# Two constant loads on another queue, conditioning sums three chunks ahead, and attention scores kept in one PSUM bank, in a two-block transformer kernel

## The chip, the core and the metric

The kernel runs as one launch on one core of one Trainium2 chip. The metric is the device time of that launch in microseconds; the median of three runs of the kernel before is 2705.99 us (2705.83 to 2706.22). Its five engines work on their own instruction streams and meet only through semaphores: TensorE (PE) for matmuls, VectorE (DVE), ScalarE (ACT), GpSimd (POOL) and the queue engine SP.

## The reference

Two transformer blocks follow each other on 256 tokens of width 2048, in fp32. The change is all in the first one. Cut to what matters:

```
mod = silu(c) @ w_ada + b_ada                      # 6 parts of 2048 ("conditioning")
shift1, scale1, gate1, shift2, scale2, gate2 = split(mod, 6)
h = rms_norm(x, norm1_w) * (1 + scale1) + shift1
u_pool, q, k, v, g_a, g_b = split(h @ w_in)        # 1024 x 4, 2048 x 2 columns
y_a = multiscale_pool(u_pool, w_pool, pool_scale) @ w_a_up
q, k = rms_norm(q, q_norm_w), rms_norm(k, k_norm_w)      # per head of 128, 8 heads
y_b = stick_breaking_attention(q, k, v) @ w_b_up
x = x + gate1 * ((sigmoid(g_a) * y_a + sigmoid(g_b) * y_b) @ w_o)
x = x + gate2 * (square(relu(h2 @ w_ff1)) @ w_ff2)       # h2: second norm and modulation

# attention of one head: z = q.k / sqrt(128), mask: key before query
log_beta = log_sigmoid(z);  l = where(mask, log_beta - z, 0)
a = where(mask, exp(log_beta + reverse_cumsum(l) - l), 0);  out = a @ v
```

## The kernel before, in words

**Weights.** All weights stream from HBM once, as pieces of 512 KB ("items"), in the order of `weight_plan`, through six slots (`RAW`, four, and `RAWX`, two). SP issues them; a slot is refilled when DVE has finished with what it held. There are two sorts. A weight chunk is 256 rows by 512 columns: ACT copies it to a rounded tile `WH` (line 993), DVE subtracts to get the rest `WL` (line 1359), and PE multiplies (line 588) with the activations, which are split the same way into `AH` and `AL`: two row blocks, two token tiles, three products each, 12 matmuls of 512 columns a chunk. `WH` and `WL` have three slots each, so ACT may copy chunk j+2 once PE is through with chunk j-1. A conditioning item is no matmul: DVE adds it, scaled by one column of silu(c), to the accumulator `ACC` (line 1367).

**Ticks.** Every engine runs one loop over the chunk number j (848 in all), and all its other work hangs at a fixed j, in the order written: on ACT and DVE `feed(j + 2)` (copies, subtractions and conditioning items up to chunk j+2), `evac` (reading out a finished PSUM bank), `quarter`, `side`; on PE the chunk and then `side`. No scheduler reorders anything: an instruction that waits holds up all that is behind it on its engine.

**The first projection** is chunks 0 to 127. Its modulation (scale1, shift1) is needed first and comes in four quarters of 512 columns. `quarter(q)` on PE sums `ACC` over partitions with two matmuls against ones; DVE takes the diagonals, adds bias and forms scale and shift (7 instructions); ACT writes `AH` of four row blocks and the unrounded values (8 instructions); `quarter_low(q)` on DVE writes `AL` (4 instructions). To have work before all quarters are there, `PIECES` splits the 16 column blocks of w_in into pieces (column block, first chunk, last chunk): first those that need only quarter 0, and so on. `SUMS` says before which chunk PE does the sum of each quarter. Before the change quarter q is summed before chunk 20, 40, 60 and first used at chunk 22, 42, 62.

**Banks.** A piece accumulates in a pair of PSUM banks (one bank for each token tile, t = 0 and 1). Column block 0 has a pair of its own until its last piece; the others alternate between two pairs. When a piece ends at chunk e, tile 0 is read out at j = e+1 and tile 1 at j = e+2 (`ended`), by ACT for a block's first piece, by DVE (as an addition) for its later ones. A piece that begins must wait for the readout of the piece that had its banks before (`bank_free`), tile by tile.

**Beside the projection**, from given chunks on: the pooling (`POOL0`); the q and k norms, whose sums of squares DVE makes, whose reciprocal roots POOL makes (`rsqrt`, 15 small dependent instructions, lines 1929 and 1934) and which DVE applies (`qk_norm`, at `QKN0`); and the attention, one head every two chunks from `STK0` on (`stick`). Stage 0 of a head transposes q and k, stage 2 makes scores Z in bank 5 and from them softplus terms on ACT and DVE (`E1`, `E2`), stage 4 makes the exponent E in bank 6: the scores again, the mask, and two matmuls that form the sums over later keys; ACT takes exp, and stage 6 multiplies with v. POOL's instruction stream holds loads as well: `ST` (the mask constants, tile `SX`) and the gate bias (1 MB, tile `G`) wait for the pooling to end and stand ahead of `rsqrt`.

Of the kernel before, what the change touches and what calls it, by code (L numbers as in the profile page):

```python
# [26 lines left out]
POOL0 = 69  # L27
QKN0 = 77
STK0 = 83
# [106 lines left out]
def weight_plan(I):  # L136
# [46 lines left out]
    head = spread(head, [ada1[2], ada1[3], ada1[4]], 62, 176)  # L183
    for q in range(1, 4):
        a, n = 20 * (q - 1), 18
# [3 lines left out]
        plan += head[a + n:a + 20]  # L189
# [105 lines left out]
class Blocks:  # L295


    def __init__(self):
# [49 lines left out]
def program(nc, I, C, out):  # L348
# [3 lines left out]
    with ExitStack() as ctx:  # L352
# [24 lines left out]
        NT = sb("NT", [128, 3, 16])  # L377
# [134 lines left out]
        s_sga, s_stat = sem("gate_a"), sem("st_landed")  # L512
# [44 lines left out]
        RSQ = {("qk", a): 15 * (a + 1) for a in range(2)}  # L557
        RSQ |= {("rope", r): 15 * (r + 3) for r in range(8)}
        RSQ |= {("mix", m): 15 * (m + 11) for m in range(4)}
        RSQ["attn"] = 15 * 15  # L560

# [23 lines left out]
        def _(e):  # L585
# [404 lines left out]
        def _(e):  # L990
# [46 lines left out]
            def evac(q, t):  # L1037
# [18 lines left out]
                elif name == "in1":  # L1056
# [3 lines left out]
                    e.wait_ge(s_stO, 8)  # L1060
# [91 lines left out]
            def stick(h, s):  # L1152
# [10 lines left out]
                elif s == 2:  # L1163
# [3 lines left out]
                    af(e1, PS[:, 5, 0:384], ACT.Abs).then_inc(s_stx, 1)  # L1167
# [4 lines left out]
                elif s == 4:  # L1172
# [3 lines left out]
                    af(e3, PS[:, 6, 0:384], ACT.Exp).then_inc(s_st3, 1)  # L1176
# [164 lines left out]
            for j in range(NW + 3):  # L1341
# [14 lines left out]
        def _(e):  # L1356
# [80 lines left out]
            def ada_made(b, g, n):  # L1437
# [183 lines left out]
            def qk_norm(a, t):  # L1621
                e.wait_ge(s_rs, RSQ["qk", a])
# [5 lines left out]
            def stick(h, s):  # L1628
                b = h % 2
                e1, e2 = E1[:, b, :], E2[:, b, :]  # L1630
                if s == 2:
# [6 lines left out]
                    stt(e2, PS[:, 5, 0:384], 0.0, e1, ALU.max, ALU.add).then_inc(s_ste, 1)  # L1638
# [180 lines left out]
            def side(j):  # L1819
# [10 lines left out]
                if j in (QKN0, QKN0 + 1, QKN0 + 5, QKN0 + 6):  # L1830
                    qk_norm((j - QKN0) // 5, (j - QKN0) % 5)
# [64 lines left out]
            for j in range(NW + 3):  # L1896
# [13 lines left out]
                if j in SUMS[1:]:  # L1910
                    quarter(SUMS.index(j))
                if j - 1 in SUMS[1:]:
                    quarter_low(SUMS.index(j - 1))
# [3 lines left out]
        def _(e):  # L1917
# [136 lines left out]
```

## Time and profile before

| what | us |
|---|---|
| median of 3 runs | 2705.99 |
| profiled execution, its own time | 2697.7 |
| its span, first to last instruction | 2695.9 |
| PE busy | 2545.9 (94%) |
| DVE busy | 2005.1 (74%) |
| ACT busy | 1271.9 (47%) |
| POOL busy | 285.3 (11%) |
| mean granted clock of TensorE | 0.981 |

Times on the timeline are microseconds from the start of the span. The first projection covers about 42 to 502 us of it. The busy time of PE counts matmuls that overlap, so a chunk of 12 matmuls that each show 0.39 us takes 2.72 us from the start of one chunk to that of the next. An fp32 matmul that is not of the rounded kind leaves two records.

### The profile page before, as it was taken

What the parts mean: (1) busy time and instruction counts of PE and PEld (TensorE: products, weight loads), DVE (VectorE), ACT (ScalarE), POOL (GpSimd) and SP (SyncE); (2) the same over time, 40 slices, a digit from 0 to 9 for tenths busy, and PEclk for the clock granted to TensorE, in tenths of its full rate; (3) what the DMA queues carried; (4) which work ended last, traced back from release to release, by engine and by line L of the source; (5) the groups of instructions that cost most, each with busy time, mean ns of one, the idle gap of its engine ahead of it and who ended that gap; (6) DMA issues with size and microseconds to landing.
All of it is one profiled execution on the core that took longest, in us unless ns stands there. A gap on an engine that the chain in (4) does not pass through costs nothing.

```text
span 2695.9 us, 36321 instructions
## 1 busy us (share of the span) xinstructions
PE 2545.9 (94%) x14339; PEld 2215.0 (82%) x14339; DVE 2005.1 (74%) x2238; ACT 1271.9 (47%) x1584; POOL 285.3 (11%) x340
## 2 busy tenths in 40 slices
PE   5999789999899999999998999978989999999998
PEld 4777678878899889988976888767789988999897
DVE  6788667899886888797887777977775566565556
ACT  4534376434454444444435554445545444444442
POOL 0000220202002020202020001461000000020000
PEclk9999899999999999999999999999999999999999
DMA  8888657988798979897965645566567777776664
GB/s 317 310 306 305 208 189 264 334 308 294 253 346 266 351 261 351 264 357 258 349 212 177 187 133 149 187 197 218 175 221 221 226 232 229 227 219 194 189 187 148
DMA packets 297882, 661.80 MB, mean 245 GB/s; under 512 B 20736, under 2 KB 20832, under 8 KB 296944
## 3 DMA queue, kind: packets, MB, share of 16 engines
q1 hardware_dynamic: 294704, 648.12, 72.6%
q0 software_dynamic: 3008, 11.36, 1.2%
q8 instruction: 114, 1.87, 0.3%
q14 instruction: 56, 0.46, 0.0%
HBM read 657.30 MB, written 2.10 MB: 245 GB/s over the span
## 4 chain that ended last, share of the span: by engine, by line
PE 77%; DVE 11%; issue 4%; ACT 4%; DMA 3%; POOL 1%; SPq 0%; DVEq 0%; ACTq 0%; POOLq 0%
PE PS L588 77%; DVE WL L1359 3%; DVE ACC L1367 3%; ACT WH L993 2%; DMA RAW<-in_w_o 1%; DVE UQ L1359 1%; DMA RAW<-in_w_in 1%; DVE hn L1364 1%; PE PS L591 0%; ACT L993 0%; ACT UQ L993 0%; DVE acc L1359 0%; DMA RAW<-in_w_out 0%; DMA RAW<-in_w_ada 0%; POOL NT L1929 0%
## 5 line engine op out<-in xcount | busy, mean ns | idle before, releaser
L1359 DVE TENSOR_TENSOR WL<-RAW,WH 128x1024 fp32r<-128x1024 f32 x573 | 714.5, 1248 | 406.9 <-ACT WH L993 405.6
L993 ACT ACTIVATE WH<-RAW 128x1024 fp32r<-128x1024 f32 x573 | 607.2, 1060 | 862.1 <-PE PS L588 665.7
L588 PE MATMUL PS<-WH,AH 128*128 128x512 f32 x2052 | 817.6, 398 | 43.3 <-DVE AL L1359 23.5
L588 PE MATMUL PS<-WH,AL 128*128 128x512 f32 x2052 | 804.3, 392 | 0.0
L588 PE MATMUL PS<-WL,AH 128*128 128x512 f32 x2052 | 804.0, 392 | 0.0
L588 PE MATMUL PS<-BH,WH 128*128 128x256 f32 x2048 | 574.8, 281 | 6.1 <-DVE BL L1359 6.1
L588 PE MATMUL PS<-BH,WL 128*128 128x256 f32 x2048 | 571.4, 279 | 0.0
L588 PE MATMUL PS<-BL,WH 128*128 128x256 f32 x2048 | 571.3, 279 | 0.0
L588 PEld LDWEIGHTS PS<-WH,AH 128*128 128x128 f32 x2052 | 389.1, 190 | 132.7 <-DVE WL L1359 31.6
L588 PEld LDWEIGHTS PS<-WH,AL 128*128 128x128 f32 x2052 | 388.2, 189 | 83.6
L588 PEld LDWEIGHTS PS<-WL,AH 128*128 128x128 f32 x2052 | 389.0, 190 | 78.8 <-issue 1.0
L588 PEld LDWEIGHTS PS<-BH,WH 128*128 128x128 f32 x2048 | 384.4, 188 | 9.7 <-DVE BL L1359 9.2
L588 PEld LDWEIGHTS PS<-BH,WL 128*128 128x128 f32 x2048 | 385.0, 188 | 0.0
L588 PEld LDWEIGHTS PS<-BL,WH 128*128 128x128 f32 x2048 | 383.1, 187 | 0.5
L1367 DVE SCALAR_TENSOR_TENSOR ACC<-RAW,CS,ACC 128x1024 f32<-128x1024 f32 x259 | 330.9, 1278 | 2.2 <-DMA RAW<-in_w_ada 1.3
L1950 POOL PARTITION_ALL_REDUCE ACC<-ACC x72 | 156.6, 2258 | 1319.8 <-DVE ACC L1367 1319.8
L993 ACT ACTIVATE WH<-RAWX 128x1024 fp32r<-128x1024 f32 x144 | 152.7, 1060 | 206.7 <-PE PS L588 137.5
L1359 DVE TENSOR_TENSOR WL<-RAWX,WH 128x1024 fp32r<-128x1024 f32 x144 | 179.5, 1247 | 60.2 <-ACT WH L993 59.6
L1359 DVE TENSOR_TENSOR WL<-RAWY,WH 128x1024 fp32r<-128x1024 f32 x96 | 117.7, 1226 | 78.8 <-ACT WH L993 78.8
L993 ACT ACTIVATE WH<-RAWY 128x1024 fp32r<-128x1024 f32 x96 | 101.9, 1062 | 137.4 <-PE PS L588 133.8
L1367 DVE SCALAR_TENSOR_TENSOR ACC<-RAWX,CS,ACC 128x1024 f32<-128x1024 f32 x101 | 128.8, 1277 | 0.9 <-DMA RAWX<-in_w_ada 0.5
L588 PE MATMUL PS<-WX,AH 128*128 128x512 f32 x248 | 78.1, 396 | 2.0 <-DVE AL L1359 2.0
(240 smaller groups left out, 2061.5 us busy)
## 6 DMA issues: line engine op xcount, KB each, us to landing
RAW<-in_w_ff SPq DMA_DIRECT2D x335, 512.0 KB, 4.5
RAW<-in_w_ada SPq DMA_DIRECT2D x278, 512.0 KB, 5.3
RAW<-in_w_in SPq DMA_DIRECT2D x197, 512.0 KB, 4.4
RAWX<-in_w_ada SPq DMA_DIRECT2D x106, 512.0 KB, 5.4
RAWY<-in_w_ff SPq DMA_DIRECT2D x96, 512.0 KB, 4.5
RAWX<-in_w_ff SPq DMA_DIRECT2D x81, 512.0 KB, 5.2
RAWX<-in_w_in SPq DMA_DIRECT2D x43, 512.0 KB, 5.3
RAW<-in_w_out SPq DMA_DIRECT2D x32, 512.0 KB, 4.6
```

The costliest lines, as they stand in the source:

```text
L588: return e.matmul(o, l, r, start=start, stop=stop, skip_group_check=True)
L993: return e.activation(o, i, f, **kw)
L1359: return e.tensor_tensor(o, a, b, op)
L1364: return e.tensor_scalar(o, a, s1, s2, op0, op1)
L1367: return e.scalar_tensor_tensor(out=o, in0=a, scalar=s, in1=b, op0=op0, op1=op1)
L1950: e.partition_all_reduce(part, part, 128, bass.bass_isa.ReduceOp.add).then_inc(s_red, 1)
```

## The change

- `PIECES` is written anew: twelve blocks instead of eleven before the second quarter is needed, 46 pieces instead of 43. Quarters are first used at chunks 24, 44 and 64 and summed before 21, 41 and 61. The conditioning items of a quarter are spread over 20 chunks instead of 18.
- At those chunks the order within an engine's turn is changed: ACT does `feed`, `quarter`, `evac` (before: `feed`, `evac`, `quarter`); DVE does `quarter`, `feed`, `quarter_low`, `evac` (before: `feed`, `evac`, `quarter`, and `quarter_low` a chunk later).
- Pooling, norms and attention start 2, 6 and 4 chunks later. POOL makes the reciprocal roots of q and k in one chain over 32 columns instead of two over 16.
- The loads of `ST` and of the first gate bias are issued by ACT (at j = 80) instead of POOL.
- In the attention the second score matmuls go: mask and sums are added to the scores in the bank where they are, and the banks alternate (5 and 6) from head to head. The mask matmuls stand behind the wait for `E2` now.

```
-POOL0 = 69
-QKN0 = 77
-STK0 = 83
+POOL0 = 71
+QKN0 = 83
+STK0 = 87
-PIECES = ([(0, 0, 2)] + [(n, 0, 2) for n in range(1, 11)]
-          + [(0, 2, 4), (11, 0, 4)] + [(n, 2, 4) for n in (7, 8, 9, 10, 1, 2, 3)]
...
+PIECES = ([(n, 0, 2) for n in range(12)]
+          + [(0, 2, 4)] + [(n, 2, 4) for n in (7, 8, 9, 10, 11, 3, 4, 5, 6)]
...
-SUMS = (0, 20, 40, 60)
+SUMS = (0, 21, 41, 61)
...
-                    if h > 0:
-                        e.wait_ge(s_ste, 2 * h)
+                    if h > 1:
+                        e.wait_ge(s_st3, h - 1)
                     mm(Z[:, 0:256], kt[:, 0:128], qt, True, False)
...
-                    mm(E[:, 0:256], kt[:, 0:128], qt, True, False)
-                    mm(E[:, 256:384], kt[:, 128:256], qt[:, 128:256], False, False)
-                    mm(E[:, 0:128], ident, neglt, False, False)
-                    mm(E[:, 256:384], ident, neglt, False, False)
                     e.wait_ge(s_ste, 2 * h + 2)
-                    mm(E[:, 0:384], nge, e2, False, False)
-                    mm(E[:, 128:256], nones, e2[:, 256:384], False, True).then_inc(s_stE, 1)
+                    mm(Z[:, 0:128], ident, neglt, False, False)
+                    mm(Z[:, 256:384], ident, neglt, False, False)
+                    mm(Z[:, 0:384], nge, e2, False, False)
+                    mm(Z[:, 128:256], nones, e2[:, 256:384], False, True).then_inc(s_stE, 1)
...
+                if j == POOL0 + 9:
+                    e.wait_ge(s_poolB, 4)
+                    e.dma_start(ST, C["st"]).then_inc(s_stat, 16)
+                    e.dma_start(G[:, :], I["b_ada"][0:1, 2 * D:3 * D].partition_broadcast(128)).then_inc(s_gb0, 16)
...
                 feed(j + look(j))
+                if j in SUMS[1:]:
+                    quarter(SUMS.index(j))
                 for q, t in bl.ended(j):
                     evac(q, t)
-                if j in SUMS[1:]:
-                    quarter(SUMS.index(j))
...
-                if j in (QKN0, QKN0 + 1, QKN0 + 5, QKN0 + 6):
-                    qk_norm((j - QKN0) // 5, (j - QKN0) % 5)
+                if QKN0 <= j < QKN0 + 4:
+                    qk_norm((j - QKN0) // 2, (j - QKN0) % 2)
...
+                    if j in SUMS[1:]:
+                        quarter(SUMS.index(j))
                     feed(j + look(j))
+                    if j in SUMS[1:]:
+                        quarter_low(SUMS.index(j))
                     for q, t in bl.ended(j):
                         evac(q, t)
...
-            for a in range(2):
-                e.wait_ge(s_msr, 4 * a + 4)
-                rsqrt(SM[:, 40 + 16 * a:56 + 16 * a], SM[:, 8 + 16 * a:24 + 16 * a], 128)
+            e.wait_ge(s_msr, 8)
+            rsqrt(SM[:, 40:72], SM[:, 8:40], 128)
```

ACT around the first of the three sums. `WH` is the copy of a chunk, `AH` and `XT` belong to the quarter, `SG<-PS` is the readout of column block 9 (first row of it tile 0, the next tile 1). Before:

```order
L993 ACTIVATE WH<-RAW 128x1024 [waits w_used,raw1_landed]
L993 ACTIVATE SG<-PS 128x512 [waits w_used]
L993 ACTIVATE AH<-XT,MOD 128x256 [waits mod_made]
...
L993 ACTIVATE XT<-XT,MOD 128x256
L993 ACTIVATE WH<-RAW 128x1024 [waits w_used,raw3_landed]
L993 ACTIVATE SG<-PS 128x512 [waits w_used]
```

Now:

```order
L989 ACTIVATE WH<-RAW 128x1024 [waits w_used,raw1_landed]
L989 ACTIVATE SG<-PS 128x512 [waits w_used]
L989 ACTIVATE WH<-RAW 128x1024 [waits w_used,raw3_landed]
L989 ACTIVATE AH<-XT,MOD 128x256 [waits mod_made]
...
L989 ACTIVATE XT<-XT,MOD 128x256
L989 ACTIVATE SG<-PS 128x512 [waits w_used]
```

The copy of the next chunk moved ahead of the quarter. The readout of tile 1 is behind the quarter in both, but the piece that takes over its banks now begins at chunk 22, one chunk after the sum; before it began at chunk 24, four chunks after the sum.

DVE around the second sum. `UQ<-PS,UQ` is the readout of a piece (before column block 2, now column block 4), `PS<-PS,SQ` begins the quarter, `AL` is `quarter_low`. Before:

```order
L1359 TENSOR_TENSOR WL<-RAW,WH 128x1024 [waits w_hi]
L1359 TENSOR_TENSOR UQ<-PS,UQ 128x512 [waits bank_read_act,w_used]
L1359 TENSOR_TENSOR PS<-PS,SQ 128x512 [waits ada_summed]
...
L1367 SCALAR_TENSOR_TENSOR MOD<-MOD,VC 128x4 [waits mod_made]
L1367 SCALAR_TENSOR_TENSOR ACC<-RAW,CS,ACC 128x1024 [waits ada_acc,raw2_landed]
L1359 TENSOR_TENSOR WL<-RAW,WH 128x1024 [waits w_hi]
L1359 TENSOR_TENSOR UQ<-PS,UQ 128x512 [waits bank_read_act,w_used]
L1359 TENSOR_TENSOR AL<-XT,AH 128x256 [waits a_hi] x4
```

Now:

```order
L1359 TENSOR_TENSOR UQ<-PS,UQ 128x512 [waits bank_read_act,w_used]
L1359 TENSOR_TENSOR PS<-PS,SQ 128x512 [waits ada_summed]
...
L1367 SCALAR_TENSOR_TENSOR MOD<-MOD,VC 128x4 [waits mod_made]
L1367 SCALAR_TENSOR_TENSOR ACC<-RAW,CS,ACC 128x1024 [waits ada_acc,raw2_landed]
L1359 TENSOR_TENSOR WL<-RAW,WH 128x1024 [waits w_hi]
L1359 TENSOR_TENSOR AL<-XT,AH 128x256 [waits a_hi] x4
L1359 TENSOR_TENSOR UQ<-PS,UQ 128x512 [waits bank_read_act,w_used]
```

The readout of tile 1 stands behind the four `AL` now. At the second and third sum the piece that takes over its banks begins at chunk 42 and 62, again one chunk after the sum.

POOL from the loads of the pooling on (`qk_sums` are the sums of squares; the instruction called ISA waits for nothing). Before:

```order
L1966 DMA SX<-const_pool 128x1536 [waits a_lo]
L1967 DMA G<-in_w_pool 128x8x256
L1969 DMA SX<-const_st 128x512 [waits pool_mapped]
L1962 DMA G<-in_b_ada 128x2048
L1929 ISA
L1929 TENSOR_SCALAR NT<-SM 128x16 [waits qk_sums]
```

Now:

```order
L1969 DMA SX<-const_pool 128x1536 [waits a_lo]
L1970 DMA G<-in_w_pool 128x8x256
L1932 ISA
L1932 TENSOR_SCALAR NT<-SM 128x32 [waits qk_sums]
```

The two loads and their wait are gone from POOL, so nothing but the sums themselves is ahead of the chain.

## Rows read from the trace of the kernel before

**Rows 1.** Stretches of the first projection: us from:to, length, busy us (instructions).

```profile
229.00:247.00 18.00, 11.58 (x40) 8.41 (x39) 13.21 (x22) 6.99 (x11) 0.00 (x0) 0.81 0.51 162
344.00:437.00 93.00, 86.77 (x431) 72.28 (x431) 53.36 (x65) 76.63 (x106) 15.34 (x8) 0.99 0.51 161
437.00:502.00 65.00, 65.00 (x288) 53.83 (x287) 58.20 (x50) 29.41 (x32) 0.00 (x0) 1.00 1.02 382
```

**Rows 2.** What PE waited for over the whole span: us, times, longest.

```profile
PE PS L588 <- DVE AL L1359: 25.5, 10, 6.4
PE PS L588 <- DVE TMP L1359: 6.2, 6, 1.8
```

**Rows 3.** PE around the first two sums: start, us, instruction [idle before].

```profile
99.09 1.88 PE L588 MATMUL PS<-ACC,SQ 128*128 128x512 f32 x4
...
111.68 0.77 PE L588 MATMUL PS<-WH,AH 128*128 128x512 f32 x1 [5.22 <-DVE AL L1359]
...
116.93 0.55 PE L588 MATMUL PS<-WH,AH 128*128 128x512 f32 x1
...
164.38 1.88 PE L588 MATMUL PS<-ACC,SQ 128*128 128x512 f32 x4
...
182.83 0.39 PE L588 MATMUL PS<-WH,AH 128*128 128x512 f32 x1
```

**Rows 4.** ACT behind the first quarter: the next copy, the readout.

```profile
108.90 1.04 ACT L993 ACTIVATE WH<-RAW 128x1024 fp32r<-128x1024 f32 x1
109.84 0.57 ACT L993 ACTIVATE SG<-PS 128x512 f32<-128x512 f32 x1
```

**Rows 5.** DVE at the first and second sum.

```profile
101.58 0.69 DVE L1359 TENSOR_TENSOR PS<-PS,SQ 128x512 f32<-128x512 f32 x1
...
177.00 0.68 DVE L1359 TENSOR_TENSOR UQ<-PS,UQ 128x512 f32<-128x512 f32 x1
177.60 1.42 DVE L1359 TENSOR_TENSOR AL<-XT,AH 128x256 fp32r<-128x256 f32 x4
```

**Rows 6.** POOL at the norms of q and k.

```profile
305.14 0.53 POOL L1962 DMA_DIRECT2D G<-in_b_ada  x1
317.56 0.19 POOL L1929 TENSOR_SCALAR NT<-SM 128x16 f32<-128x16 f32 x1 [11.89 <-issue]
...
322.07 1.16 POOL L1929 TENSOR_SCALAR NT<-SM 128x16 f32<-128x16 f32 x1 [0.17 <-POOL SM L1934]
...
335.93 0.22 POOL L1934 TENSOR_TENSOR SM<-NT 128x16 f32<-128x16 f32 x1
```

**Rows 7.** DVE there: the last sum of squares and the first norm.

```profile
302.50 0.67 DVE L1370 TENSOR_REDUCE SM<-TMP 128x4 f32<-128x512 f32 x1
...
321.94 1.22 DVE L1359 TENSOR_TENSOR UQ<-UQ,SM 128x1024 f32<-128x1024 f32 x1 [14.42 <-POOL SM L1934]
```

**Rows 8.** PE there: first matmuls of chunks 79, 80, 84, 85, and the first transposes.

```profile
309.59 0.39 PE L588 MATMUL PS<-WH,AH 128*128 128x512 f32 x1
...
325.55 0.79 PE L588 MATMUL PS<-WH,AH 128*128 128x512 f32 x1 [13.08 <-DVE WL L1359]
...
343.06 1.12 PE L591 MATMUL PS<-SQ,UQ 128*128 128x128 f32 x4 [4.47 <-DVE UQ L1359]
343.82 0.78 PE L588 MATMUL PS<-WH,AH 128*128 128x512 f32 x1
...
347.66 0.40 PE L588 MATMUL PS<-WH,AH 128*128 128x512 f32 x1
```

**Rows 9.** DMA issue of the gate biases: queue, count, KB, us to landing.

```profile
G<-in_b_ada POOLq DMA_DIRECT2D x1, 1024.0 KB, 8.8
```

**Rows 10.** PE in one turn of the attention: scores again, mask, sums, next scores.

```profile
377.32 0.82 PE L588 MATMUL PS<-UQ 128*128 128x256 f32 x4
377.98 0.61 PE L588 MATMUL PS<-SX,SQ 128*128 128x128 f32 x4
380.38 1.13 PE L588 MATMUL PS<-TMP,SX 128*128 128x384 f32 x4 [1.79 <-DVE TMP L1359]
```

More of the change, by code:

```diff
@@ L35 @@
 GM0 = 544
-PIECES = ([(0, 0, 2)] + [(n, 0, 2) for n in range(1, 11)]
-          + [(0, 2, 4), (11, 0, 4)] + [(n, 2, 4) for n in (7, 8, 9, 10, 1, 2, 3)]
-          + [(0, 4, 6)] + [(n, 2, 6) for n in (4, 5, 6)] + [(n, 4, 6) for n in (1, 2, 3)]
-          + [(0, 6, 8)] + [(n, 6, 8) for n in range(1, 7)] + [(n, 4, 8) for n in range(7, 12)]
+PIECES = ([(n, 0, 2) for n in range(12)]
+          + [(0, 2, 4)] + [(n, 2, 4) for n in (7, 8, 9, 10, 11, 3, 4, 5, 6)]
+          + [(0, 4, 6)] + [(n, 2, 6) for n in (1, 2)] + [(n, 4, 6) for n in (3, 4, 5, 6, 7)]
+          + [(0, 6, 8)] + [(n, 6, 8) for n in range(1, 8)] + [(n, 4, 8) for n in range(8, 12)]
           + [(n, 0, 8) for n in range(12, 16)])
-SUMS = (0, 20, 40, 60)
+SUMS = (0, 21, 41, 61)
 CONST_SQ = ["ident", "ones"]
@@ L182, in weight_plan @@
     plan += quarter[0]
-    head = spread(head, [ada1[2], ada1[3], ada1[4]], 62, 176)
+    head = spread(head, [ada1[2], ada1[3], ada1[4]], 64, 178)
     for q in range(1, 4):
-        a, n = 20 * (q - 1), 18
+        a, n = 20 * (q - 1), 20
         for i in range(n):
@@ L188, in weight_plan @@
             plan += quarter[q][16 * i // n:16 * (i + 1) // n]
-        plan += head[a + n:a + 20]
     plan += head[60:]
@@ L309, in __init__ @@
             else:
-                b = 2 * (pair % 2) + (2 if at < 62 else 0)
+                b = 2 * (pair % 2) + (2 if at < 64 else 0)
                 pair += 1
@@ L376, in program @@
         SS = sb("SS", [128, 13])
-        NT = sb("NT", [128, 3, 16])
+        NT = sb("NT", [128, 3, 32])
         ident, ones = SQ[:, 0:128], SQ[:, 128:256]
@@ L511, in program @@
         s_red = sem("ada_reduced")
-        s_sga, s_stat = sem("gate_a"), sem("st_landed")
+        s_sga, s_stat, s_gb0 = sem("gate_a"), sem("st_landed"), sem("first_gbias_landed")
         s_cs, s_vecT, s_vc = sem("silu_c"), sem("vec_turned"), sem("vec_copied")
@@ L556, in program @@
                 cols[b, g] = mods
[L557 to L560, printed above, removed]
+        RSQ = {"qk": 15}
+        RSQ |= {("rope", r): 15 * (r + 2) for r in range(8)}
+        RSQ |= {("mix", m): 15 * (m + 10) for m in range(4)}
+        RSQ["attn"] = 15 * 14
         def x_count(name, n, t):
@@ L700, in stick @@
                 qk, e2, e3 = QKT[:, h % 2, :], E2[:, h % 2, :], E3[:, h % 2, :]
-                T, Z, E, O = PS[:, 4, :], PS[:, 5, :], PS[:, 6, :], PS[:, 7, :]
+                T, Z, O = PS[:, 4, :], PS[:, 5 + h % 2, :], PS[:, 7, :]
                 kt, qt = qk[:, 256:512], qk[:, 0:256]
@@ L1166, in stick @@
                         e.wait_ge(s_ste, 2 * h - 2)
-                    af(e1, PS[:, 5, 0:384], ACT.Abs).then_inc(s_stx, 1)
+                    af(e1, PS[:, 5 + b, 0:384], ACT.Abs).then_inc(s_stx, 1)
                     e.wait_ge(s_stx, 3 * h + 1)
@@ L1175, in stick @@
                         e.wait_ge(s_stO, h - 1)
-                    af(e3, PS[:, 6, 0:384], ACT.Exp).then_inc(s_st3, 1)
+                    af(e3, PS[:, 5 + b, 0:384], ACT.Exp).then_inc(s_st3, 1)
                 elif s == 6:
@@ L1446, in ada_made @@
                     if n == 0:
-                        e.wait_ge(s_gb, 16 * (gates[b, g] // 4 + 1))
+                        if (b, g) == (0, 2):
+                            e.wait_ge(s_gb0, 16)
+                        else:
+                            e.wait_ge(s_gb, 4 * gates[b, g])
                     tt(G[:, cols_n], part, G[:, cols_n], ALU.add).then_inc(s_g, 1)
@@ L1621, in qk_norm @@
             def qk_norm(a, t):
-                e.wait_ge(s_rs, RSQ["qk", a])
+                e.wait_ge(s_rs, RSQ["qk"])
                 v = heads(UQ[:, a + 1, t, :])
@@ L1637, in stick @@
                         e.wait_ge(s_stE, h - 1)
-                    stt(e2, PS[:, 5, 0:384], 0.0, e1, ALU.max, ALU.add).then_inc(s_ste, 1)
+                    stt(e2, PS[:, 5 + b, 0:384], 0.0, e1, ALU.max, ALU.add).then_inc(s_ste, 1)
                     d = e2.rearrange("p (a t) -> p a t", t=128)[:, 0:3:2, :]
@@ L1825, in side @@
                     for t in range(2):
-                        if j == 2 * n + 65 + t:
+                        if j == 2 * n + 67 + t:
                             i = 2 * (n - 2) + t + 1
@@ L1906, in _ @@
                 else:
+                    if j in SUMS[1:]:
+                        quarter(SUMS.index(j))
                     feed(j + look(j))
+                    if j in SUMS[1:]:
+                        quarter_low(SUMS.index(j))
                     for q, t in bl.ended(j):
                         evac(q, t)
[L1910 to L1913, printed above, removed]
                 side(j)
```

6 lines of the change are left out of this document (removed).

## The prediction

> **What bounds the kernel now.** I read the busy shares first, then the stretches of the first projection, PE's waits, and then the timelines around each wait. PE is busy 94% of the span, so what the change can give is PE's idle time and PE's own work, between chunk 20 and the end of the attention. In quiet stretches PE is at 65.00 of 65.00 us and the DMA engines carry 382 GB/s beside it; around a sum PE has 11.58 of 18.00 us at a granted clock of 0.81 [rows 1]. A quiet chunk takes 2.72 us: (502 - 437)/2.72 is 24 chunks. PE's longest waits are for `AL` (25.5 us in ten), one of 13.08 us and one of 4.47 us at the norms of q and k, and 6.2 us in six for the attention's `E2` [rows 2, 8]. Each is followed by a stretch at half speed, the lower of the two clock levels.
>
> **The three sums.** Call T the start of PE's sum. Before, three chunks were done at T + 17.84 at the first sum (99.09 to 116.93) and T + 18.45 at the second (164.38 to 182.83); the third repeats the second [rows 3]. Of the 17.84 us, 5.22 us is the wait and three chunks and the sum are 7.37 + 2.72 (PE fell idle at 111.68 - 5.22 = 106.46, which is T + 7.37, after the sum and two chunks); 2.53 us is left for the slow clock. At the second the wait is 6.42 us and the same sum leaves 1.94 us.
>
> Now three chunks lie between sum and use, so the wait for `AL` should go. But at chunks 22, 42 and 62, after one chunk only, a piece begins in the banks of one that ended three chunks earlier. Its tile 1 is read out behind the quarter (ACT, first sum) or behind the four `AL` (DVE, the others). What stands in front: DVE can start at about T + 0.95 (half of the 1.88 us of the four records, an estimate) [rows 3]; from DVE's first instruction of the quarter to ACT's next copy took 101.58 to 108.90, 7.32 us [rows 4, 5]; that is T + 8.3. Readout by ACT 0.57: T + 8.9. By DVE: one `AL` (1.42/4 = 0.36) and 0.68: T + 9.4 [rows 5]. PE arrives at tile 1 of the new piece at T + 7.37 - 2.72 + 0.68 (three matmuls of 0.227) = T + 5.3. So PE waits 3.6 us at the first sum and 4.1 us at the others, in the middle of a chunk. Nine matmuls (2.04) and a chunk (2.72) follow, and I take 1.9 us for the slow clock, as at the second sum before: three chunks done at T + 15.6, T + 16.1, T + 16.1. Against 17.84, 18.45, 18.45 that is 2.2 + 2.4 + 2.4 = **7.0 us less**. The copies for chunk 24 come after the readout, at about T + 11.2, and PE wants them at T + 12.9 or later: hidden. Bounds: 1.5 us less (DVE starts its quarter as late as before, T + 2.5, at each) and 23 us less (no bank wait; see the rivals).
>
> **The norms of q and k.** Before, POOL issued the 1 MB bias at 305.14 and did its first step at 317.56; DVE stood 14.42 us for the result, and PE 13.08 us because DVE made no `WL` [rows 6 to 8]. From chunk 79 to the first transposes 33.47 us passed for five chunks (309.59 to 343.06), 19.9 more than 5 x 2.72. Behind the transposes chunk 84 took 3.84 us, 1.1 too much, and they themselves 0.4 too much [rows 8]. In all 21.4 us.
>
> Now POOL has nothing in front of the chain. The last sum of squares comes at the counterpart of 302.50 + 0.67 (everything there is two chunks later, pieces and pooling alike). The first norm stands at j = 83. I simulated DVE from chunk 80 on, in its written order: 1.14 for `WL`, 1.2 for a conditioning item (two at one chunk), 0.6 for a readout, 1.15 for a norm. It reaches the first norm at the counterpart of 319.5, so POOL has 16.4 us. The chain beside an idle DVE took 4.4 us (317.56 to 321.94), beside a busy one 14.1 us (322.07 to 336.15) [rows 6, 7]. I take 14.1: it fits, by 2.3 us. Four norms in four chunks make 3.5 to 4.1 us of DVE work each against 2.72 of PE; DVE's lead of some 3 us absorbs the most, and at the first transposes PE waits 3.9 us. I add 1.0 us of slow clock and 0.5 us for the two loads. 21.4 - 5.4 = **16.0 us less**. Bounds: 21.4 (all hidden), and 8 (chain 17.7 us, loads fully on the path, slow clock of 2.5).
>
> The loads are 1.31 MB, 3.4 us of the DMA engines at 382 GB/s [rows 1, 9]. DVE-bound chunks leave them free meanwhile, hence the 0.5. ACT's issue of two loads is not in this trace; the nearest row is POOL's own, 0.53 us, and ACT is idle more than 1 us a chunk: nothing. What it may cost at most is the last rival.
>
> The first step of the second chain took 1.16 us, that of the first, beside an idle DVE, 0.19 [rows 6]. If each of the 15 steps were held for one DVE instruction of 1.2 us, the chain would take 18 us and DVE would wait 1.6 us at the norm; that is part of the third case below. The Trainium skill, "SBUF — State Buffer", section "Who interferes with whom", states such a rule: a GpSimd instruction that reads SBUF is blocked for the whole of a VectorE instruction with two SBUF inputs. By that, the trace agrees for the first step, and by the whole chain's 14.1 us not every step meets such an instruction.
>
> **The attention.** In its 93 us PE is busy 86.77 and ACT 76.63, with waits in a ring: PE for DVE's `E2`, DVE for ACT's logarithm, ACT for DVE's readouts [rows 1, 2]. The second score matmuls take 377.98 - 377.32 = 0.66 us a head, 5.2 us in all [rows 10]. Where PE then waits (six heads of eight), they were done inside that time and only lengthen the wait; the mask matmuls (0.45 us a head, estimated from the 0.61 of the row less the overlap) now stand behind it. So the edit by itself is worth between 5.2 us less and 6 x 0.45 = 2.7 us more; I take 1. The four-chunk shift puts heads beside other work: two turns of about 10 us lose ACT's sigmoid with its table load or DVE's conditioning items, and the sigmoid of column block 12 falls into the last ones. I take 2.5 us less for that (0 to 4). **3.5 us less.**
>
> **The rest.** Three more pieces are six more readouts of 0.6 us on DVE and ACT, beside PE's matmuls; two conditioning items move from chunk 104 to the end of the run at 177, where DVE is nearly full: **0.5 us more** (0 to 3).
>
> **Sum.** 7.0 + 16.0 + 3.5 - 0.5 = 26.0 us less. The profiled execution took 2697.7 us (span 2695.9) and would take 2671.7; it is 8.3 us under the median of the runs. The forecast is for a median: 2706.0 - 26.0 = **2680 us**.
>
> **The rivals.**
> 1. *As above*, 2680.
> 2. *The readout does not hold PE* (or the clock does not fall after a wait of 4 us). Then chunk 24 waits only for its own `WL`: T + 8.3, a copy of 1.04 and a subtraction of 1.2, T + 10.6, instead of 15.6 or 16.1. That is 16 us less, 2664; with the bank wait but full clock 2680 - 5.7 = 2674. For it: PE did not arrive sooner at the third chunk in any row, so the bank wait itself is not in this trace. Against it: the order of instructions leaves no other way for that readout, and 4.47 us cost 1.1 us [rows 8].
> 3. *Crowding at chunks 80 to 88.* POOL's chain is late by 1.6 us, the loads cost their 3.4 us on PE, the clock stays low for 2.5 us: 7.5 less the 1.5 I have, 2686; with DVE's backlog reaching the first turns of the attention 2688. For it: DVE has more work a chunk there than PE. Against it: the 3 us of lead, and DMA engines that wait for DVE. The Trainium skill, "DMA: Bandwidth & Descriptors", section "Issuing engines are not separate DMA queues", says that loads of all issuers share the same 16 engines; so moving them to ACT's queue buys no bandwidth.
> 4. *The attention is held by ACT and DVE alone*: nothing of its 3.5 us comes and the mask adds 2.7: 2686.
> 5. *Slower: ACT is held while it issues.* POOL stood 11.89 us behind its issue of the bias, and that load needed 8.8 us to land [rows 6, 9]. If ACT were held for both with each of the two loads, 41.4 us, no `WH` would be made; PE has one chunk of 2.7 us in hand: 38.7 us on the path, 2719. It decides from 26 + 2.7 = 28.7 us of hold. Against it: SP issues loads of 512 KB one or two to a chunk without such gaps.
>
> **How the numbers follow.** Chances: case 1 0.51, case 2 with its milder form 0.15, case 3 0.19, case 4 0.11, case 5 0.04. The range of 8 in 10 takes in cases 1, 3, 4 and the milder half of case 2: 2666 to 2692. 0.2% (5.4 us) is about what a measurement can tell from no change; only case 5, or several terms at their far ends, comes near it: faster 0.94, same 0.02, slower 0.04.
>
> **What would show it.** In the profile after: PE's waits for `AL` in the projection reduced to the first, and in their place three waits of 3.5 to 4.5 us inside chunks 22, 42 and 62 whose releaser is a readout (ACT `SG`, then DVE `UQ`), with the clock still low behind them; POOL's chain begun within a microsecond of the last sum of squares and lasting about 14 us; no 13 us wait; one wait of 2 to 4 us before the first transposes; PE's waits for `TMP` in the attention longer, not shorter, than 1.79 us. If there is no wait inside chunks 22, 42 and 62, my first term is wrong; if the norm on DVE waits for POOL, the second is.

## The result, and the profile after

The changed kernel took 2691.95 us (median; 2687.62 to 2693.68) beside 2705.91 us (2702.79 to 2706.22) for the kernel before on the same chip. The ratio is 0.9949, 95% interval 0.9931 to 0.9966: 14 us less, not the 26 us forecast, and at the upper edge of the forecast's range.

The head of the kernel did what the prediction said. First PE's waits over the span, after (columns as in [rows 2]):

```profile
PE PS L587 <- DVE UQ L1359: 8.6, 2, 4.3
PE PS L587 <- DVE AL L1359: 7.5, 7, 3.6
PE PS L587 <- DVE TMP L1359: 7.5, 5, 2.7
```

and, in the stretch from 0 to 300 us alone, the readout on ACT:

```profile
PE PS L587 <- ACT SG L989: 3.7, 1, 3.7
```

The three waits for `AL` behind the sums are gone (25.5 us over the whole span in [rows 2], 7.5 now, of which 3.6 is the first quarter's), and three waits for a readout stand in their place, with the releasers that were named. PE's timeline after: the first sum, the wait inside chunk 22, one matmul at the slow clock (0.63 us long in place of 0.39), the start of chunk 24; then the same at the second sum, with the start of chunk 44; chunk 66; and at the end the first transposes, chunks 88 and 89 (compare [rows 3, 8]):

```profile
102.09 1.88 PE L587 MATMUL PS<-ACC,SQ 128*128 128x512 f32 x4
...
111.11 0.50 PE L587 MATMUL PS<-WH,AH 128*128 128x512 f32 x1 [3.69 <-ACT SG L989]
...
112.68 0.63 PE L587 MATMUL PS<-WH,AH 128*128 128x512 f32 x1
...
117.63 0.39 PE L587 MATMUL PS<-WH,AH 128*128 128x512 f32 x1
...
165.07 1.88 PE L587 MATMUL PS<-ACC,SQ 128*128 128x512 f32 x4
...
174.67 0.79 PE L587 MATMUL PS<-WH,AH 128*128 128x512 f32 x1 [4.28 <-DVE UQ L1359]
...
182.42 0.39 PE L587 MATMUL PS<-WH,AH 128*128 128x512 f32 x1
...
250.80 0.39 PE L587 MATMUL PS<-WH,AH 128*128 128x512 f32 x1
...
309.81 0.39 PE L587 MATMUL PS<-WH,AH 128*128 128x512 f32 x1
...
333.08 0.66 PE L590 MATMUL PS<-SQ,UQ 128*128 128x128 f32 x4 [2.19 <-DVE UQ L1359]
333.50 0.47 PE L587 MATMUL PS<-WH,AH 128*128 128x512 f32 x1
...
337.91 0.40 PE L587 MATMUL PS<-WH,AH 128*128 128x512 f32 x1
```

309.81 is chunk 81, the counterpart of chunk 79 in [rows 8]. POOL after, from the first to the last step of the one chain (compare [rows 6]): it begins at the last sum of squares, not 11.89 us behind two issues.

```profile
303.51 2.30 POOL L1932 TENSOR_SCALAR NT<-SM 128x32 f32<-128x32 f32 x1 [127.71 <-DVE SM L1370]
...
307.46 2.78 POOL L1937 TENSOR_TENSOR NT<-NT 128x32 f32<-128x32 f32 x3
...
313.65 0.26 POOL L1937 TENSOR_TENSOR SM<-NT 128x32 f32<-128x32 f32 x1
```

ACT after, where it issues the two loads (ACTq is its sequencer), and the copies around them:

```profile
307.35 1.06 ACT L989 ACTIVATE WH<-RAW 128x1024 fp32r<-128x1024 f32 x1
307.37 0.38 ACTq L1289 DMA_DIRECT2D SX<-const_st  x1
307.78 0.45 ACTq L1290 DMA_DIRECT2D G<-in_b_ada  x1
310.07 1.06 ACT L989 ACTIVATE WH<-RAWX 128x1024 fp32r<-128x1024 f32 x1 [1.66 <-PE PS L587]
```

It issued both beside a copy that was running and was not held. Its next three copies waited 4.26, 1.52 and 1.67 us for their weights to land; DVE stood only 0.30 and 0.16 us behind them, so PE hardly felt it. Whether the two loads delayed these weights isn't told apart. By the start of chunk 108 (447.66 us before, 424.56 after) the change was 23.1 us ahead. It did not stay so. ACT's copies of weights mark chunks 656, 720 and 847 of the feed-forwards, first in the kernel before, then after:

```profile
2150.02 1.06 ACT L993 ACTIVATE WH<-RAW 128x1024 fp32r<-128x1024 f32 x1 [1.77 <-PE PS L588]
...
2327.59 1.06 ACT L993 ACTIVATE WH<-RAW 128x1024 fp32r<-128x1024 f32 x1 [1.76 <-PE PS L588]
...
2678.52 1.06 ACT L993 ACTIVATE WH<-RAW 128x1024 fp32r<-128x1024 f32 x1 [1.66 <-PE PS L588]
```

```profile
2141.23 1.06 ACT L989 ACTIVATE WH<-RAW 128x1024 fp32r<-128x1024 f32 x1 [1.82 <-PE PS L587]
...
2320.47 1.06 ACT L989 ACTIVATE WH<-RAW 128x1024 fp32r<-128x1024 f32 x1 [1.82 <-PE PS L587]
...
2674.00 1.06 ACT L989 ACTIVATE WH<-RAW 128x1024 fp32r<-128x1024 f32 x1 [1.66 <-PE PS L587]
```

From chunk 656 to 720 before took 177.57 us and after 179.24, 1.67 more. 32 of these chunks are matmuls of 256 columns, 24 to a chunk, and 32 of 512 columns, which keep their 2.722 us; so a chunk of the first kind takes 0.052 us more (2.827 before, 2.879 after). The kernel has 256 of them: 13.4 us. (A matmul of the first kind loads 128 columns of `WH` or `WL` and streams 256 of `BH` or `BL`; most of the second kind load `AH` and stream `WH`.) Yet PE has no gap in either; a 22 us window inside such a stretch, before and then after (columns as in [rows 1]):

```profile
2290.00:2312.00 22.00, 22.00 (x189) 22.00 (x188) 12.69 (x13) 8.79 (x9) 0.00 (x0) 1.00 0.72 219
```

```profile
2290.00:2312.00 22.00, 22.00 (x186) 22.00 (x185) 12.28 (x11) 10.88 (x14) 0.00 (x0) 1.00 0.74 227
```

Busy throughout, clock 1.00, 189 matmuls against 186. The only other trace of it is the page's row of these matmuls and of their weight loads, in the kernel before:

```profile
L588 PE MATMUL PS<-BH,WH 128*128 128x256 f32 x2048 | 574.8, 281 | 6.1 <-DVE BL L1359 6.1
...
L588 PEld LDWEIGHTS PS<-BH,WH 128*128 128x128 f32 x2048 | 384.4, 188 | 9.7 <-DVE BL L1359 9.2
```

and after:

```profile
L587 PE MATMUL PS<-BH,WH 128*128 128x256 f32 x2048 | 582.9, 285 | 5.1 <-DVE BL L1359 5.1
...
L587 PEld LDWEIGHTS PS<-BH,WH 128*128 128x128 f32 x2048 | 395.1, 193 | 8.7 <-DVE BL L1359 8.2
```

Elsewhere other matmuls became faster. Chunks 128 to 159 load `BH` and stream 512 columns of `WH`. In 23 of these chunks PE has no gap; the first and the last of their 276 matmuls, before and then after:

```profile
502.06 0.40 PE L588 MATMUL PS<-WH,BH 128*128 128x512 f32 x1
...
566.23 0.39 PE L588 MATMUL PS<-WH,BL 128*128 128x512 f32 x1
```

```profile
479.07 0.39 PE L587 MATMUL PS<-WH,BH 128*128 128x512 f32 x1
...
541.40 0.39 PE L587 MATMUL PS<-WH,BL 128*128 128x512 f32 x1
```

That is 0.2333 us from one start to the next before and 0.2267 after, with PE busy throughout at a granted clock of 1.00 in both. Over the 384 matmuls of these 32 chunks it gives back 2.5 us. 372 matmuls of the second block load `AH` or `AL` and stream `WX`, a fourth slot for weights; from start to start they took 0.2305 us before and 0.2281 after, 0.9 us in all. So the net loss is 13.4 - 3.4 = 10.0 us.

Behind chunk 192, where the first feed-forward begins, 13.4 - 0.9 = 12.5 us of it should be lost. ACT's copies for chunk 192 were at 683.47 and 660.01 us, so the lead fell from 23.5 to 4.5 us, by 19.0. Beside the second profile of the kernel before (e4 below, copies for chunks 192 and 847 at 683.44 and 2684.31) it fell from 23.4 to 10.3, by 13.1. Those two executions of one kernel differ by 5.8 us between chunks 192 and 656, at the same pace of the feed-forwards; the cause of that isn't known.

### The profile page after: what moved, and what is told of

It reads as the page before. It is cut to its first block, busy times and chain, and to the rows that moved or that the text cites. A ratio compares the mean times of both kernels' runs of the same rounds, so it can differ in the third digit from the quotient of the medians.

```text
span 2691.3 us, 36253 instructions
## 1 busy us (share of the span) xinstructions
PE 2554.0 (95%) x14307; PEld 2226.6 (83%) x14307; DVE 2007.0 (75%) x2244; ACT 1272.1 (47%) x1584; POOL 279.9 (10%) x323
## 4 chain that ended last, share of the span: by engine, by line
PE 77%; DVE 10%; issue 4%; ACT 4%; DMA 3%; POOL 1%; SPq 0%; DVEq 0%; ACTq 0%
PE PS L587 77%; DVE WL L1359 3%; DVE ACC L1367 3%; ACT WH L989 1%; DVE UQ L1359 1%; DMA RAW<-in_w_in 1%; DVE hn L1364 1%; DMA RAW<-in_w_ff 0%; PE PS L590 0%; ACT L989 0%; DMA RAW<-in_w_o 0%; ACT UQ L989 0%; DMA RAWX<-in_w_o 0%; DMA RAW<-in_w_out 0%; DMA RAW<-in_w_ada 0%
## 5 line engine op out<-in xcount | busy, mean ns | idle before, releaser
L1359 DVE TENSOR_TENSOR WL<-RAW,WH 128x1024 fp32r<-128x1024 f32 x567 | 706.0, 1246 | 402.4 <-ACT WH L989 401.0
L587 PE MATMUL PS<-BH,WH 128*128 128x256 f32 x2048 | 582.9, 285 | 5.1 <-DVE BL L1359 5.1
L587 PE MATMUL PS<-BL,WH 128*128 128x256 f32 x2048 | 581.4, 284 | 0.0
L587 PE MATMUL PS<-BH,WL 128*128 128x256 f32 x2048 | 581.4, 284 | 0.0
L587 PEld LDWEIGHTS PS<-WH,AH 128*128 128x128 f32 x2052 | 389.5, 190 | 117.4 <-DVE WL L1359 16.1
L587 PEld LDWEIGHTS PS<-BH,WH 128*128 128x128 f32 x2048 | 395.1, 193 | 8.7 <-DVE BL L1359 8.2
L587 PEld LDWEIGHTS PS<-BL,WH 128*128 128x128 f32 x2048 | 395.0, 193 | 0.5
L587 PEld LDWEIGHTS PS<-BH,WL 128*128 128x128 f32 x2048 | 395.0, 193 | 0.0
L1367 DVE SCALAR_TENSOR_TENSOR ACC<-RAW,CS,ACC 128x1024 f32<-128x1024 f32 x265 | 338.6, 1279 | 1.3 <-DMA RAW<-in_w_ada 0.4
L1359 DVE TENSOR_TENSOR WL<-RAWX,WH 128x1024 fp32r<-128x1024 f32 x150 | 186.4, 1243 | 64.0 <-ACT WH L989 63.0
L1367 DVE SCALAR_TENSOR_TENSOR ACC<-RAWX,CS,ACC 128x1024 f32<-128x1024 f32 x95 | 121.5, 1279 | 0.4
```

The lines of the kernel that those rows point to most:

```text
L587: return e.matmul(o, l, r, start=start, stop=stop, skip_group_check=True)
L1359: return e.tensor_tensor(o, a, b, op)
L1367: return e.scalar_tensor_tensor(out=o, in0=a, scalar=s, in1=b, op0=op0, op1=op1)
```

## The experiments

The suspect in the diff is `NT`, 16 columns wider in each of three rows: 192 bytes a partition. `RAWX`, `BH` and `BL` are allocated behind it and start 192 bytes later; `RAW`, `WH`, `WL`, `AH`, `AL` lie ahead of it and stay. Below, "distance" is the start of `BH` less that of `WH`, modulo 128 bytes. From the buffers' sizes it is 135104 - 32896, which leaves 64, before, and 135296 - 32896, which leaves 0, after. `RAW`, `WL`, `AH` and `AL` share `WH`'s remainder; `BL` shares that of `BH`, and so does `WX`, which is allocated behind `NT` too.

**e1_before_nt32.** The kernel before, with this alone:

```diff
-        NT = sb("NT", [128, 3, 16])
+        NT = sb("NT", [128, 3, 32])
```

> The kernel before with one number changed: NT has 32 columns a third instead of 16, as in the changed kernel, and only 16 are used; everything allocated behind it, BH and BL of the feed-forward among it, starts 192 bytes later in each partition (BH at 135296 instead of 135104). Theory 'address': the 256-column matmuls of both feed-forwards go from 0.118 to 0.120 us apart, the erosion seen behind chunk 192 (about 19 us over 6144 matmuls) comes from that alone, and this kernel is 15 to 20 us slower than the one before. Rival 'execution': the pace of these matmuls differs from one execution to the next whatever the program; then this kernel takes the same time within 4 us and its pace is anything between 0.118 and 0.120. Rival 'program': the pace follows from the changed instruction stream; then here 0.118 and the same time.

Measured: 2712.64 us beside 2704.24, ratio 1.0034 (1.0023 to 1.0046). From chunk 656 to 720 it takes 179.24 us, the same as after. A wider scratch buffer that nothing reads more of makes the kernel slower by 9 us (6 to 12). The matmuls that load `BH` and stream `WH` took 0.2267 us here too, and those of `WX` 0.2279, so the 10 us worked out above is what it should cost.

**e2_after_pad.** The changed kernel, with a buffer behind `NT` that nobody uses; distance 64:

```diff
         NT = sb("NT", [128, 3, 32])
+        PAD = sb("PAD", [128, 16])
```

> The changed kernel with 64 bytes a partition left unused behind NT, so that BH and BL start 256 bytes later than in the kernel before (135360), at the same place within 128 and 256 bytes. Theory 'address': pace 0.118 us, the 23 us gained up to chunk 192 stay to the end, 22 to 26 us faster than before. Rival 'execution' or 'program': as the changed kernel, 12 to 16 us faster, pace not tied to this.

Measured: 2679.25 us (2675.12 to 2680.69), ratio 0.9904 (0.9891 to 0.9918). 177.57 us from chunk 656 to 720, as before. That is 26 us (22 to 29) less than before, the forecast's figure, and 12 us better than the changed kernel by the ratios (0.9904 and 0.9949), where the paces give 10.0.

**e4_before_again.** The kernel before once more, with its profile.

> The kernel before once more, for a second profile. Theory 'address': 0.118 us between the 256-column matmuls, chunk for chunk as in the first profile. Rival 'execution': another pace.

Measured: 2703.51 us. The pace is 2.827 us again and 177.58 us from chunk 656 to 720, so it belongs to the program, not to the execution; the whole is 5.8 us longer than in the first profile (2697.7).

**e8_shift_all, e9_pad_32, e10_pad_96, e11_pad_192, e12_shift_both.** The changed kernel with pads of other sizes, and with a pad of 64 bytes ahead of all buffers, which moves `WH` too:

```diff
+        PAD = sb("PAD", [128, 16])
         RAW = sb("RAW", [128, 4, 1024])
```

> The changed kernel with 64 bytes of pad ahead of the first buffer, so that weights, activations and the second operand of the feed-forwards all start 64 bytes later (remainders by 128: WH 64, AH 64, BH 64, where the changed kernel has 0, 0, 0 and the kernel before 0, 0, 64). Theory A (the start of BH and BL alone sets the pace of the 256-column matmuls): feed-forward chunks at 2.827 us as before, 2680 us. Theory B (it is the distance of the operand to the weights that counts): 2.879 us a chunk as in the changed kernel, 2692 us.

> The changed kernel with 32 bytes of pad behind NT: RAWX, BH and BL start 32 bytes later (BH at remainder 32 by 128, in place of 0; the kernel before has 64). Theory A (only a start at a multiple of 128 bytes is slow): the feed-forwards' 256-column chunks at 2.827 us, as before, some 13 us less than the changed kernel, about 2680. Theory B (only a remainder of 64 is fast): 2.88 us a chunk, 2692. Theory C (the pace goes by steps with the start): something between.

> The changed kernel with 96 bytes of pad behind NT (BH at remainder 96 by 128). Theory A: 2.827 us a chunk, about 2680; theory B: 2.88 us a chunk, about 2692; theory C: between.

> The changed kernel with 192 bytes of pad behind NT (BH at remainder 64 by 128, as in the kernel before, but the other half of 256: with 64 bytes of pad BH stands at 192 by 256 or at 64, and here at the other). If the remainder by 128 decides: 2.827 us a chunk, about 2680; if the one by 256: 2.88 us, about 2692.

> The changed kernel with 64 bytes of pad ahead of the first buffer and 64 more behind NT: WH starts at remainder 64 by 128, BH at remainder 0, their distance is 64 by 128 as in the kernel before. Theory B (the distance of the two starts decides): 2.827 us a feed-forward chunk of 256-column matmuls, about 2680 us. Rival (a multiple of 128 is slow for BH, and a WH off a multiple is slow as well): 2.88 us, about 2693.

Measured, with the start of `WH` and `BH` modulo 128. The column "us a chunk" is for chunks of 256-column matmuls; the two behind it are ns from one start to the next, over the 276 matmuls that load `BH` and stream `WH` and over those that load `AH` and stream `WX` (`WX` less `AH` leaves the same distance):

| kernel | WH | BH | distance | us a chunk | ns, `BH` loaded | ns, `WX` streamed | us |
|---|---|---|---|---|---|---|---|
| before | 0 | 64 | 64 | 2.827 | 233.3 | 230.5 | 2705.91 |
| after | 0 | 0 | 0 | 2.879 | 226.7 | 228.1 | 2691.95 |
| e8_shift_all | 64 | 64 | 0 | 2.879 | 226.7 | 228.1 | 2694.64 |
| e9_pad_32 | 0 | 32 | 32 | 2.800 | 233.3 | 233.5 | 2677.43 |
| e2_after_pad | 0 | 64 | 64 | 2.827 | 233.3 | 230.4 | 2679.25 |
| e11_pad_192 | 0 | 64 | 64 | 2.827 | 228.9 | 233.3 | 2674.89 |
| e12_shift_both | 64 | 0 | 64 | 2.827 | 233.3 | 230.5 | 2681.44 |
| e10_pad_96 | 0 | 96 | 96 | 2.880 | 234.3 | 234.0 | 2692.62 |

The same row of the page, in e8_shift_all:

```profile
L588 PE MATMUL PS<-BH,WH 128*128 128x256 f32 x2048 | 581.7, 284 | 5.3 <-DVE BL L1360 5.3
```

in e12_shift_both:

```profile
L589 PE MATMUL PS<-BH,WH 128*128 128x256 f32 x2048 | 576.6, 282 | 5.7 <-DVE BL L1361 5.7
```

e8 has `BH` where a start is fast and is slow; e12 has `BH` where it is slow after the change, and is fast. The start of `BH` alone does not decide, the distance does. It is not monotone: for the 256-column matmuls 32 is the fastest, 96 as slow as 0. Of e9's expectations, the one that only a multiple of 128 is slow fell with e10, and the one that only 64 is fast with e9 itself. The paces are those of the second block's feed-forward, worked out from ACT's copies of weights; before, after and e2_after_pad stand with their medians, the others with a single run.

The 512-column matmuls of the two columns in ns go another way: a distance of 0 is their fastest, with e8 (0) beside after and e12 (64) beside before, so for them as well the distance counts and not the start. Modulo 128 is not the whole of it for them. e11 and e2_after_pad, both at 64, differ (228.9 and 233.3 ns, 233.3 and 230.4 ns); modulo 256 their distances are 192 and 64.

**e5_act_loads.** The kernel before, with the two loads, and the wait for the pooling in front of them, moved to ACT's queue:

```diff
+                if j == POOL0 + 9:
+                    e.wait_ge(s_poolB, 4)
+                    e.dma_start(ST, C["st"]).then_inc(s_stat, 16)
+                    e.dma_start(G[:, :], I["b_ada"][0:1, 2 * D:3 * D].partition_broadcast(128)).then_inc(s_gb0, 16)
...
-            e.wait_ge(s_poolB, 4)
-            e.dma_start(ST, C["st"]).then_inc(s_stat, 16)
-            gate_bias("b_ada", 2)
```

> The kernel before, with one part of the change alone: the ST table and the gate bias are loaded from ScalarE's queue (at its chunk 78, behind its fourth split) and GpSimd goes straight to its chain for the norms; the two chains of 15 stay, and so do the places of all sums, norms and the attention (NT keeps its 16 columns). Theory (the GpSimd queue stood 11.89 us because it issued these loads; the chain in the way of the norms starts that much earlier, and TensorE's norm wait of 13 us goes as far as the two chains of 5.4 and 7 us, taken one behind the other, do not hold it themselves): 5 to 11 us faster than before, 2695 to 2700. Rival (the 11.89 us had another cause, such as the chain's first row waiting behind contention on the queue, and the gain of the change in this stage came from the due times moved): the chain starts no earlier, no change within 2 us.

Measured: 2690.36 us beside 2702.20, ratio 0.9955 (0.9942 to 0.9968): 12 us, a little more than expected. POOL's timeline in it, the first steps of its two chains and the last:

```profile
282.84 1.15 POOL L1936 TENSOR_SCALAR NT<-SM 128x16 f32<-128x16 f32 x1 [102.00 <-DVE SM L1374]
...
303.06 2.30 POOL L1936 TENSOR_SCALAR NT<-SM 128x16 f32<-128x16 f32 x1 [14.07 <-DVE SM L1374]
...
315.64 1.12 POOL L1941 TENSOR_TENSOR SM<-NT 128x16 f32<-128x16 f32 x1
```

Both chains start with their sums of squares; the first runs 34.7 us earlier than before (282.84, and 317.56 in [rows 6]). PE's wait of 13.08 us is gone, and the one for the first transposes is 4.50 us, as before. But the edit took two things from in front of the chain. Before, POOL stood at the wait for the pooling until 304.60, ahead of the first load:

```profile
304.60 0.56 POOL L1969 DMA_DIRECT2D SX<-const_st  x1 [123.79 <-PE PS L588]
```

The other 11.89 us come behind the second load. The wait for the pooling alone would have cost little, as DVE came to the first norm at 307.52 (321.94 less its wait of 14.42) and a chain took 4.4 us before (317.56 to 321.94) and 6.2 us here (282.84 to 288.99): 1.5 to 3.3 us at the first norm, an estimate from these rows. So most of the gain comes from the 11.89 us. What they were isn't shown: the issue of the loads, their landing, or the instruction called ISA, which stands between the loads and the chain, waits for nothing and has no row in any profile. Here and in the changed kernel it has over 100 us of idle time ahead of the chain in which to run.

**e3_evac_first.** The changed kernel, with the readouts ahead of the sum's quarter on ACT and DVE (DVE's edit is the same):

```diff
-                if j in SUMS[1:]:
-                    quarter(SUMS.index(j))
                 for q, t in bl.ended(j):
                     evac(q, t)
+                if j in SUMS[1:]:
+                    quarter(SUMS.index(j))
```

> The changed kernel with the readouts put ahead of the quarter at the three sums, on ACT and on DVE; nothing else. Theory: the waits of 3.7, 4.3 and 4.3 us inside chunks 22, 42 and 62 vanish, and with them the slow clock behind them; what is left is at most 1 us each before chunks 24, 44, 64. By the prediction's own sum of that case 16 us less than the changed kernel; from the trace after (waits 12.3 us, slow clock about 5.5 us) 12 to 17 us. Rival: the wait only moves to WL of chunk 24 or to AL, as before the change: under 6 us less.

Measured: 2684.82 us, ratio 0.9928 (0.9916 to 0.9941), beside the changed kernel's 0.9949. PE's timeline in it at the first sum, and at chunk 66:

```profile
102.02 1.88 PE L587 MATMUL PS<-ACC,SQ 128*128 128x512 f32 x4
...
113.36 0.50 PE L587 MATMUL PS<-WH,AH 128*128 128x512 f32 x1 [1.25 <-DVE WL L1359]
...
239.34 0.47 PE L587 MATMUL PS<-WH,AH 128*128 128x512 f32 x1 [0.61 <-DVE UQ L1359]
```

The bank waits are gone and chunk 24 starts at T + 11.3 in place of T + 15.5, close to the prediction's second case (T + 10.6). At chunk 66 it is 11.5 us ahead of the changed kernel (239.34 against 250.80). Then 5.4 us come back, 3.4 of them in chunks 66 to 71 (21.5 us against 18.2), with a wait for a readout of 1.90 us in chunk 66 and a lower granted clock (0.96 against 1.00 from there to chunk 88). At chunk 108 6.0 us are left (418.52 against 424.56). Neither expectation was right alone: half of what the bank waits cost moved on.

**e6_scores_twice.** e2_after_pad, with the scores multiplied a second time into a bank of their own:

```diff
+                    mm(E[:, 0:256], kt[:, 0:128], qt, True, False)
+                    mm(E[:, 256:384], kt[:, 128:256], qt[:, 128:256], False, False)
```

> The changed kernel with 64 bytes of pad behind NT (as in e2_after_pad, 2679.25 us there), and with the attention's edit undone: the scores are multiplied again into a bank of their own (two matmuls of 256 and 128 columns for each of the 8 heads, some 0.2 us a head at full clock), each head's matmuls wait as before. Theory (attention edit is worth the 16 removed matmuls and the waits around them, 2.4 to 3.5 us): 2.0 to 4.0 us slower than e2_after_pad, about 2682. Rival (the longer waits of TensorE for TMP in the changed kernel, 7.5 us against 6.2, give the gain back): within 1 us of e2_after_pad.

Measured: 2681.94 us, ratio 0.9927 (0.9915 to 0.9939), against 0.9904 for e2_after_pad. By the timelines it loses 2.5 us up to the copy for chunk 128 (478.69 us against 476.15) and 1.8 us to the end. The edit gives about 2 us; the ratios allow 1 to 11.

**e7_best and e13_best32.** Pad and early readouts together; in the second the pad is 32 bytes.

> The changed kernel with both improvements that the experiments so far point to: 64 bytes of pad behind NT (e2_after_pad gained 13.2 us with it) and the readouts of a finished pair ahead of the sum's quarter on ScalarE and VectorE at the three sums (e3_evac_first: 6.6 us less than the changed kernel at the head's end). Theory (they act in different stages and add up): 2672 to 2674 us, ratio to before about 0.988. Rival (the second only moves waits, which come back at later places): within 2 us of e2_after_pad's 2679.

> The kernel of e7_best (readouts ahead of the quarter, pad behind NT) with the pad at 32 bytes in place of 64: distance of BH to WH 32 by 128. Theory B and the pace of e9_pad_32 (2.800 us a chunk against 2.827): 256 chunks x 0.027 = 6.8 us less than e7_best, ratio to before about 0.987, 2668 us. Rival (the 2.800 of e9_pad_32 was that execution alone): the same as e7_best, ratio 0.990.

Measured: e7_best 2674.88 us, ratio 0.9899 (0.9887 to 0.9912); e13_best32 2670.94 us, ratio 0.9889 (0.9871 to 0.9906). Both beat both kernels. That e7_best beats e2_after_pad (0.9904) can't be told by the ratios; in the timelines it is 5.1 us ahead at the end (2656.09 against 2661.18 at the copy for chunk 847). e13 has the pace of 2.800 us a chunk again, 0.027 less than e7; by that 6.8 us, less 1.1 for the matmuls that stream `WX` (233.5 ns apiece, 230.4 in e7). The medians show 4, the two profiles 9.7 at the copy for chunk 847 (2646.41 and 2656.09).

## Why the prediction was wrong

**The three sums, -7.0.** Right in mechanism: waits of 3.69, 4.28 and 4.29 us where 3.6, 4.1 and 4.1 were worked out. Three chunks were done at T + 15.5, T + 17.3 and T + 16.0 (forecast 15.6, 16.1, 16.1); the second kept the low clock longer. At chunk 66 the gain is 255.77 - 250.80 = 5.0 us.

**The norms, -16.0.** Right. From chunk 81 to the transposes 333.08 - 309.81 = 23.27 us passed for seven chunks (19.04), 4.2 too much; chunk 88 took 4.41 us, 1.7 too much, and the transposes 0.1. 6.0 us are left of 21.4, so 15.4 us gained. The wait at the transposes was 2.19 us where 3.9 was forecast. The chain took 10.4 us (303.51 to 313.91) in place of 14.1 and did not matter: DVE began the first norm at 320.21, 6.3 us after its end. Its single steps took from 0.22 to 2.30 us beside a busy DVE. By the Trainium skill, "SBUF — State Buffer", section "Who interferes with whom", a GpSimd instruction that reads SBUF is blocked for the whole of a VectorE instruction with two SBUF inputs; by that the trace agrees for the long steps, and again not for all fifteen. e5 shows that taking the loads and the wait in front of them off POOL gives 12 us by itself.

**The attention, -3.5.** 2.4 us: from chunk 88 to 108 91.06 us, of which 1.7 is the slow clock at its start, against 92.84 with 1.1 from chunk 84 to 104 before. PE's waits for `TMP` became longer, 2.7 us at most in place of 1.79, as said.

**The rest, +0.5.** This is the step that failed. It counted readouts and conditioning, and said nothing of `NT = sb("NT", [128, 3, 32])`, which is in the diff. The edit has no instruction, so no row of the profile before carries it; but it moves every buffer behind it, and with them the operands of 6144 matmuls that follow each other without a gap for a quarter of the span (256 chunks of 2.83 us). e1 shows its cost alone (+9 us, 6 to 12) and e2 its removal (2679.25 us against 2691.95). The paces give 13.4 us lost by the 256-column matmuls and 3.4 gained by 756 of the 512-column ones, 10.0 us net. The other three terms measured 5.0 + 15.4 + 2.4 = 22.8 us where 7.0 + 16.0 + 3.5 = 26.5 were forecast, so they came 3.7 us short as well; with the 10.0 the sum is 12.8 us, against 14 measured (9 to 19). What the six readouts and two conditioning items of this term cost wasn't separated. That e2 hits the forecast's 26 us is in part luck: it has the same three terms, and its interval is 22 to 29.

Of the rivals none came true. The fifth, that ACT is held while it issues, is excluded by the copies at 307.35 and 310.07. Of the third's crowding only a little was there: PE waited 0.19 and 1.04 us for `WL` and 2.19 us at the transposes. At chunk 108 the three terms' 22.8 us stand beside 23.1 us measured.

## What to carry to other kernels

An edit of a buffer's size is an edit of the place of all buffers behind it: price it, where a bound engine reads them, by comparing the rate of the same matmuls in a stretch without gaps, and try pads of 32 and 64 bytes. Look at every kind of matmul that reads them, since here the distance that was fastest for one kind was slow for another. Follow a gain through landmarks over the whole span; a loss spread over 256 chunks at 0.05 us each shows in no list of waits. Where a sum is moved ahead of its use, look for what else its engines owe in those chunks: the readouts behind it held PE by 4 us, three times.

## What the runs showed of the hardware

Back-to-back fp32r matmuls of 256 columns, each with its own weight load, ran at 0.1167, 0.1178 or 0.1200 us apiece (2.800, 2.827, 2.879 us for 24), all at full clock and with PE shown busy throughout. Which it is went by the distance of the start of the moving operand's and the weights' buffers modulo 128 bytes: 32, 64, and 0 or 96 (e9, e2 and e12, after, e8 and e10). Here 128 columns of `WH` or `WL` are loaded and 256 of `BH` or `BL` stream through; which of the two reads is slowed isn't told apart.

Back-to-back matmuls of 512 columns that load `BH` and stream `WH` ran at 0.2267 us at a distance of 0 and at 0.2333 us at 32 and at 64 (0.2289 in e11), again at full clock without a gap. Those that stream `WX` and load `AH` ran at 0.228 us at 0, 0.230 at 64 and 0.233 to 0.234 at 32, at 96 and in e11. Most matmuls of 512 columns load `AH` and stream `WH`, whose distance is 0 in every run; they kept 0.2268 us (2.722 us a chunk). `RAW`, `WH`, `WL`, `AH` and `AL` share one remainder in every run, so that the distance is to the other operand, and not to another of these buffers, is inferred from what the matmuls read. The cause behind the distance stays open.

A step of GpSimd's chain in the changed kernel, from 303.51 to 305.81 us, took 2.30 us beside two VectorE instructions with two SBUF inputs each, the second of which ended at 305.74; a later step of the same width, at 313.35, took 0.22 us.
